# Block products as pairs of 64 by 64 tiles in a recurrent mixer, and level products of a gated recurrence issued one step later

## What is computed

```python
def step(state, inp):
    r_t, w_t, k_t, v_t, a_t, b_t = inp
    sa = jnp.einsum('bhvk,bhk->bhv', state, a_t)
    state = (state * w_t[:, :, None, :] + sa[..., None] * b_t[:, :, None, :]
             + v_t[..., None] * k_t[:, :, None, :])
    return state, jnp.einsum('bhvk,bhk->bhv', state, r_t)
```

## Time and profile before

| | us |
|---|---|
| median of three runs (lowest, highest) | 2407.83 (2401.4, 2412.27) |
| profiled execution, its own time | 2398.57 |
| span of the profiled execution | 2396.8 |
| PE busy in it | 2364.5 (99%) |
| DVE, ACT, POOL busy | 1660.5, 1274.0, 384.4 |

### The profile page before, as it was taken

One profiled execution on the slowest core, in us unless ns is written; L12 is line 12 of the kernel. 1 busy time (PEld: TensorE's weight loads), 2 busy tenths in 40 slices (PEclk: granted clock), 3 DMA queues, 4 the chain that ended last, 5 costly groups with the idle time before them and its releaser, 6 DMA issues.

```text
span 2396.8 us, 50331 instructions
## 1 busy us (share of the span) xinstructions
PE 2364.5 (99%) x21468; PEld 2299.1 (96%) x21468; DVE 1660.5 (69%) x2312; ACT 1274.0 (53%) x1816; POOL 384.4 (16%) x327
## 2 busy tenths in 40 slices
PE   9999999999999999999999999999999999999998
PEld 9999889999999999899999999989999999989998
DVE  7775776966667657878666765776666666777664
ACT  6554656645445456565554444655554454655553
POOL 4012020300200210203003002521002002521001
PEclk9999999999999999999999999999999999999999
DMA  7555433555555554245554555412555555412553
GB/s 256 188 194 192 159 126 137 178 194 193 189 183 193 192 178 174 107 142 186 199 192 179 220 194 195 155 53 103 199 194 183 198 188 193 164 57 90 211 188 129
DMA packets 57679, 410.18 MB, mean 171 GB/s; under 512 B 6384, under 2 KB 6640, under 8 KB 8688
## 3 DMA queue, kind: packets, MB, share of 16 engines
q1 hardware_dynamic: 56592, 402.15, 46.4%
q10 hardware_dynamic: 864, 4.82, 0.6%
HBM read 405.89 MB, written 1.05 MB: 170 GB/s over the span
## 4 chain that ended last, share of the span: by engine, by line
PE 88%; DVE 6%; ACT 3%; issue 2%; DMA 0%; DVEq 0%; SPq 0%; POOL 0%; POOLq 0%; ACTq 0%
PE bank L301 87%; DVE area L314 3%; ACT area L310 3%; DVE sb_wlo L314 2%; PE bank L305 1%; DVE area L342 1%; ACT sb_whi L310 0%; DVE area L325 0%; ACT L310 0%; DMA sb_x<-x 0%; DVE area L352 0%; DVE sb_x L325 0%; DVE area L320 0%; DVE area L319 0%; DVE sb_x L314 0%
## 5 line engine op out<-in xcount | busy, mean ns | idle before, releaser
L301 PE MATMUL bank<-area,sb_whi 128*128 128x256 f32 x11752 | 2041.3, 279 | 5.2 <-ACT area L310 3.1
L301 PEld LDWEIGHTS bank<-area,sb_whi 128*128 128x128 f32 x11752 | 1781.1, 188 | 17.7 <-ACT area L310 5.2
L301 PE MATMUL bank<-area,sb_wlo 128*128 128x256 f32 x5876 | 1620.2, 278 | 4.1 <-DVE sb_wlo L314 4.0
L310 ACT ACTIVATE sb_whi<-sb_raw 128x1024 fp32r<-128x1024 f32 x762 | 799.7, 1057 | 710.3 <-PE bank L301 705.8
L301 PEld LDWEIGHTS bank<-area,sb_wlo 128*128 128x128 f32 x5876 | 1101.1, 188 | 5.6 <-DVE sb_wlo L314 5.6
L314 DVE TENSOR_TENSOR sb_wlo<-sb_raw,sb_whi 128x1024 fp32r<-128x1024 f32 x762 | 962.4, 1272 | 166.1 <-ACT sb_whi L310 164.6
L314 DVE TENSOR_TENSOR area<-area,area 128x256 f32<-128x256 f32 (+6 forms) x502 | 257.9, 523 | 233.4 <-ACT area L310 231.9
L310 ACT ACTIVATE area<-area 128x256 f32<-128x256 f32 (+6 forms) x515 | 252.3, 498 | 81.9 <-DVE area L314 63.2
L314 DVE TENSOR_TENSOR area<-bank,sb_x_diag 128x512 f32<-128x512 f32 x244 | 166.8, 684 | 31.4 <-PE bank L301 18.8
L301 PE MATMUL bank<-area,area 64*64 64x64 f32 (+4 forms) x2496 | 154.9, 248 | 8.3 <-ACT area L310 6.0
L301 PEld LDWEIGHTS bank<-area,area 64*64 64x64 f32 (+3 forms) x2496 | 130.8, 149 | 28.3 <-ACT area L310 9.6
(11 more groups left out here) (82 smaller groups left out, 704.2 us busy)
## 6 DMA issues: line engine op xcount, KB each, us to landing
sb_raw<-stream SPq DMA_DIRECT2D x379, 1024.0 KB, 4.8
sb_raw<-stream SPq DMA_DIRECT2D x4, 512.0 KB, 7.7
area<-lora ACTq DMA_DIRECT2D x2, 768.0 KB, 4.8
area<-c ACTq DMA_DIRECT2D x1, 1504.0 KB, 8.4
sb_x<-x SPq DMA_DIRECT2D x4, 256.0 KB, 5.8
area<-mem ACTq DMA_DIRECT2D x1, 1024.0 KB, 7.2
out<-sb_x SPq DMA_DIRECT2D x4, 256.0 KB, 2.9
area<-m ACTq DMA_DIRECT2D x1, 512.0 KB, 3.7
```

The source lines that it names most:

```text
L301: return lambda e: e.matmul(out, lhsT, rhs, start=start, stop=stop, skip_group_check=True, tile_position=at)
L310: return lambda e: e.activation(out, a, f, **kw)
```

## The change

Every block-diagonal operand goes. `own_head` multiplies the two halves of the partitions apart, as 64 by 64 tiles at rows and columns 0 and 64, both into the same PSUM bank, on the lower and the upper half of its partitions. The clears on POOL, the copies onto diagonals on ACT and the pairs of half-height operations on DVE go with the arrays. `rwkv_inverse` starts with the pending evacuation (`settle`) and with bank 3 (`m.turns = 0`), and the transposes of `at` move from its start into its first two rounds, on bank 7. In the first mixer the level products of a step are issued in the next step, behind its values and ahead of its filler; the four scalings of `decays` move to `k.later`; the sum `soft` moves from POOL to DVE.

```diff
@@ attend
+    products = None
     for s in range(14):
...
         if 0 <= s - 2 < 12:
             values_of(s - 2)
+        if products:
+            products()
         if s < 12:
             exponentials(s, n)
...
         fill(k)
-        if products:
-            products()
@@ recurrence
+        def lowered():
+            dve.wait(pool, w.clipped)
+            dve.wait(act, n2)
+            for h in range(4):
+                w.lowered = dve.mark(tensor_scalar(z[:, h, :], zp[:, h, :], -1.0, ALU.mult,
...
+        k.later.extend((exponentials, logs, lowered))
     def decays():
-        dve.wait(pool, w.clipped)
...
-        pool.wait(dve, w.c_start)
-        w.soft = pool.mark(tensor_tensor(flat(zp), flat(zp), flat(e1), ALU.add))
+        def soft():
+            w.soft = dve.mark(tensor_tensor(flat(zp), flat(zp), flat(e1), ALU.add))
+        k.later.append(soft)
@@ the new helper
+def own_head(k, out, lhsT, rhs, start=True):
+    for e in range(2):
+        r = half_of(e)
+        n = k.pe.mark(matmul(out[r], lhsT[r], rhs[r], start=start, stop=True, at=(64 * e, 64 * e)))
     return n
@@ wide_products
-        n = k.pe.mark(matmul(k.bank[b][:, 128 * j:128 * j + 128], lhs[:, 4 * i + j, :], rhs[:, 4 * i + j, :]))
+        g = 4 * i + j
+        n = own_head(k, k.bank[b][:, 128 * j:128 * j + 128], lhs(g), rhs[:, g, :])
@@ rwkv_inverse
+    settle(k)
+    m.turns = 0
...
-        for e in range(2):
-            n = dve.mark(tensor_tensor(m.ak_d[half_of(e), groups(i), half_of(e)], broad(k, b)[half_of(e), :, 64:128],
-                                       wide(const2(k, "lower"), 4)[half_of(e)], ALU.mult))
+        done["ak"] = dve.mark(tensor_tensor(m.ak[:, groups(i), :], broad(k, b)[:, :, 64:128],
+                                            wide(const2(k, "lower"), 4), ALU.mult))
...
-    rwkv_by_token(k, m, m.at, m.a_tm_d, done["at"], "a_tm")
     for n in range(1, 6):
...
+        if n <= 2:
+            pe.wait(*m.freed[7])
+            done["a_tm"] = rwkv_by_token(k, k.bank[7], n - 1, m.at, m.a_tm)
+            m.freed[7] = (act, done["a_tm"])
         fill(k, 1)
...
-            if n < 5:
-                x_done[h] = dve.mark(tensor_tensor(by_row(xx, h), product, by_row(xx, h), ALU.add))
-            else:
-                for e in range(2):
...
+            x_done[h] = dve.mark(tensor_tensor(by_row(xx, h), product, by_row(xx, h), ALU.add))
@@ rwkv_chunks
         s_done = act.mark(activation(flat(m.st[i]), b[:, 0:256], ACT.Copy))
...
-        act.wait(act, s_done)
-        for e, r in enumerate(rows_):
-            d_done = act.mark(activation(m.st_d[r, groups(i), 64 * e:64 * e + 64], m.st[i][r], ACT.Copy))
...
-        pe.wait(act, d_done)
+        pe.wait(act, s_done)
```

More of the change, by code:

```diff
@@ L2061, in rwkv_prepare @@
     first[0](first[1])
-    pool.wait(pe, before)
-    for a in m.diag[:3]:
-        clear(a)
     two("k", kk, 2, 8)
@@ L2246, in rwkv_prepare @@
     flush_later(k)
-    act.wait(pool, w.cleared)
-    rwkv_by_token(k, m, v, m.v_tm_d, done["v", 2], "v_tm", center=True)
+    pe.wait(dve, done["v", 2])
+    for tt in range(2):
+        u = side_bank(k, m)
+        done["v_tm"] = rwkv_by_token(k, k.bank[u], tt, v, m.v_tm, center=True)
+        m.freed[u] = (act, done["v_tm"])
     bonus_products()
-    k.later.extend((k_diagonal, bonus, rotate))
+    k.later.extend((bonus, rotate))
     plain(k, m, ("rg", 0), m.rg[:, 0:2, :])
@@ L2253, in rwkv_prepare, with rwkv_by_token @@
     flush_later(k)
[L2255 to L2277, removed]
+def rwkv_by_token(k, bank, tt, src, dst, center=False):
+    for j in range(4):
+        to, block = bank[:, 128 * j:128 * j + 128], src[:, j, 128 * tt:128 * tt + 128]
+        n = k.pe.mark(matmul(to, block, const(k, "center")) if center else transpose(to, block, const(k, "ident")))
+    k.act.wait(k.pe, n)
+    for c in range(2):
+        for e in range(2):
+            read = bank[half_of(c)].rearrange("p (j c) -> p j c", j=4)[:, :, half_of(e)]
+            n = k.act.mark(activation(dst[half_of(e), groups(2 * tt + c), :], read, ACT.Copy))
+    return n
 def rwkv_products(k, m, name, i, unit=False):
@@ L2301, in rwkv_inverse @@
     x_done, t_done, w_done, a_done = {}, {}, {}, {}
-    at_of = lambda g: m.at[:, g % 4, 64 * (g // 4):64 * (g // 4) + 64]
+    settle(k)
+    m.turns = 0
     dve.wait(k.c2_slot, k.c2_in)
-    pe.wait(act, max(done["bt", "d"], done["at", "d"]))
-    dve.wait(pool, max(m.cleared, done["xx"]))
+    pe.wait(dve, max(done["bt"], done["at"], done["kt"]))
+    dve.wait(pool, done["xx"])
     for h in range(2):
         b = side_bank(k, m)
-        n = block_products(k, b, h, m.bt_d, at_of)
+        for o in range(8):
+            g = 8 * h + o
+            n = own_head(k, k.bank[b][:, 64 * o:64 * o + 64], m.bk[:, g, 0:64], at_of(m, g))
         dve.wait(pe, n)
@@ L2417, in own @@
             o = 64 * (4 * (i % 2) + j)
-            in_halves(k, ys[i // 2][:, o:o + 64], m.v_tm_d[:, 4 * i + j, :], m.rk[:, 4 * i + j, 0:64],
-                      start=i % 2 == 0 and j == 0, stop=False)
+            own_head(k, ys[i // 2][:, o:o + 64], m.v_tm[:, 4 * i + j, :], m.rk[:, 4 * i + j, 0:64],
+                     start=i % 2 == 0 and j == 0)
     def squares(h, bank, n):
```

85 lines of the change are left out of this document (23 added, 62 removed).

## The result

The changed kernel takes 2376.76 us in the median of four executions (2376.17 to 2378.21), the kernel before 2410.05 in as many (2401.40 to 2413.69). The ratio is 0.9876, with a 95% interval of 0.985 to 0.9902: faster by 1.2%. The forecast was faster, but by 17 us, and its range ended at 2382; the kernel gained 33 us. The profiled execution, at 2377.26 us with a span of 2375.5, is 21.3 us under the one of before.

A forecast was written before the change was run, and what follows sets the result against it. PE, busy 99% of the span, was taken as the bound, so only its waits could be won: 5.4 + 2.5 + 9.0 = 16.9 us off 2407.8 gives 2391 us, range 2382 to 2408.

The forecast's parts named there:

- Part 3: Start of the inverse, second mixer: two PE waits cost 1.8 us, 0.25 left for bank 7, gain 1.5 us a layer.
- level products: First mixer: issuing them one step later removes all eight PE waits on DVE ahead of them, gain 5.4 us.
- decays: First mixer: moving scalings and the sum removes PE's 1.10 us wait for a weights split in two layers, gain 2.5 us.
- second mixer: Start and end of the inverse plus the chain: 4.5 us a layer, 9.0 us for both layers.
- the second rival: Waits return at values or a split in the first mixer: 11.5 us gain stays, 2396 us, chance 0.16.
- the case that I called the worst: At `decays`, the sum on DVE stays beside the two splits: DVE needs 3.7 us in place of 4.2.
- Parts 3 and 4: Second mixer: start of the inverse 1.5 us, its end 1.2, the chain 1.7; together 4.5 us a layer.
- Part 5: Second mixer's 64 by 64 tiles: no gain, no loss taken; upper bound 57.7 us if tiles run in turn.
- The chain: Chain behind the inverse: dropping ACT's two copies shortens two PE waits of 0.93 us, gain 1.7 us a layer.
- the work taken from POOL and ACT: POOL's clears and ACT work away from the priced places: counted as nothing, since PE waits for neither there.
- The rival of tiles in turn: Two tiles of one product in one bank take turns: +57.7 - 16.9 = +41 us, 2449 us, chance 0.12.

The follow-up runs named there:

- E4: Kernel before with only the decays edits (four scalings moved to `k.later`, sum `soft` on DVE): 2404.14 us median (2396.22 to 2415.00).
- E6: Kernel before with only the new start of the inverse, all block-diagonal arrays kept: twelve executions between 2396.07 and 2399.11 us.
- E10: Changed kernel plus six ACT copies that the first round's second quarter products wait for: four executions at 2379.37 to 2380.51 us, two at 2385.45 and 2386.64.
- E2: Kernel before with only the first mixer's edits (level products a step later, scalings to `k.later`, sum on DVE): 2392.22 us median, profile span 2387.8.
- E3: Kernel before with only the second mixer's edits (64 by 64 tiles, no block-diagonal arrays, new order of the inverse): 2388.01 us, span 2385.2.
- E5: Changed kernel with the old start of the inverse, 64 by 64 tiles kept: five executions 2384.51 to 2390.37 us; a sixth, 4821.82 us, left out.
- E7: Changed kernel with two ACT copies behind every state of the chain put back, for which PE waits: 2380.99 us (2380.66 to 2383.76).
- E11: Changed kernel plus four ACT copies that the first round's second quarter products wait for: five executions between 2377.96 and 2379.15 us.

## Why the prediction was wrong

**The step that failed is the price of the waits in Part 3.** It made the two waits at the inverse's start 1.8 us, their idle time and the overlap, and took the clock as 1.00 because the one profile showed that. Half of the executions of before (39 of 79) have a mean clock of 0.996 or less. In E4's trace of such an execution the engine fell to 1.2 GHz from about there, and the same work took 6 and 9 us more in the two layers. E6 took away the second of these waits and left 0.65 us of the first kind, and the executions of low clock went; E10 put a wait of 1.26 us in the second one's place, and two of six returned. The sum of the forecast was made against an execution of full clock and then set off the median of executions that, by their times, mostly weren't. So the 33.3 us between the medians are 21.3 between the profiles, and 11.5 by which the median of before (2410.05) lies over its profile (2398.57); 0.5 is the change's own (2377.26 to 2376.76). The size of the 11.5 is luck: over the 79 executions the median lies 3.4 us over that profile. The range failed with this step: its lower end counted all idle time, and a fall of the clock isn't idle.

**The terms between executions of full clock** were right in place in the main, level products and second mixer too small:

| | forecast | measured by |
|---|---|---|
| level products | 5.4 | 6.5: E2's span (9.0) less decays |
| decays | 2.5 | 2 x 1.27: dense products around the place |
| second mixer | 9.0 | 12.6: dense products ahead of and behind the two mixers, before and after |
| sum | 16.9 | 21.6; 21.3 from profile to profile |

E3's span shows 11.6 for the second mixer, since its profiled execution lost 2 us in its first 60 us, where the two kernels do the same.

*Level products:* seven of the eight waits went; the last is 0.23 us where it was 0.30. In addition steps without a wait got 0.3 us shorter (one from 3.57 to 3.28 us between a low part of one filler and a low part of the next, at 318 and 317 us), likely because the products now start beside the last values. What the second rival named, waits that come back at a split, happened on a small scale: 1.0 us in three waits of the second layer. E2 has them too, E4 not, so they come with the level products.

*Decays:* as forecast, in the case that I called the worst: the sum does stand between the splits, and DVE is early enough. PE had waited for the first of the two slow splits, which alone took 3.07 us.

*Second mixer:* the stretch over the inverse fell from 49.8 to 46.3 us, 3.5 where Parts 3 and 4 have 1.5 + 1.2. The waits of the earlier trace rows at both ends went: 1.8 + 0.8 + 0.4, less 0.43 for bank 7, where 0.25 was left: 2.6. Bank 7 was thus dearer than Part 3 allowed. Of the other 0.9 a part is Part 5, where I excluded a gain: the tiles are cheaper by 0.004 us a group, and, it seems, tiles of one size follow each other without the pause that a change of size makes: the group products ahead of the rounds took 9.43 us in the timeline of before (128 records) and 9.07 in E5's (192 records for the same). What is left of the 0.9 wasn't followed. The chain gave 1.78 for 1.74 (E7). Some 0.5 us a layer was won ahead of the inverse, between dense products, where the forecast put the work taken from POOL and ACT at nothing; in the third layer a wait of 0.30 us for a split, at 1540.25 us, is gone there. Why was not tested.

**The rival of tiles in turn fell** with the first trace: 0.219 us a group, twice that by that rival. The rule on row tiles and banks that I weighed in Part 5 doesn't hold for tiles on different halves of the partitions of a bank; the measurement decides. It fits a sentence of another page of the Trainium skill, "PSUM — Partial Sum Buffer", section "PSUM bank collisions raise a hardware error", which says that each bank in each partition is a memory of its own; the same section also repeats the rule that fell here. Row halves in one bank and on the same partitions weren't tried.

**Still open:** why the clock falls in some executions and not in others of the same kernel, and whether the first wait of 0.49 us has a share in it beside the second. E5 had one wait of 1.73 us and a low clock in five executions of five, though in its trace in only one of the two layers; before has 0.49 and 1.16 and a low clock in half, E10 0.36 and 1.26 and in two of six, E11 0.36 and 0.39 in none of five, E6 one wait of 0.65 in none of twelve.

## What to carry to other kernels

When the timed executions of a kernel spread and its profile sits at the fast end, look at the granted clock of every execution before summing waits: the profile may be of the kind that doesn't show the cost. A wait of a microsecond between small tiles can cost several times its idle time (E10: 1.26 us, and some 6 more in two of six executions); two waits of 0.93 us in the chain (E7) cost no more than the forecast's 1.74. Block-diagonal operands are not needed to keep two small heads side by side: here two tiles on the diagonal cost PE no more (0.219 us a group for 0.223) and spare the other engines the zeros.

## What the runs showed of the hardware

- In the traces of E4 and E5 the clock fell to 1.2 GHz within 3 us behind a wait of 1.16 to 1.73 us, on an engine that was 99% busy, and stayed there for 10 to 20 us; behind a like wait in E5's fourth layer it did not. With waits of 0.39 us (E11) or 0.65 us (E6) at the start of the rounds no execution showed a low clock.
- Two tiles of 64 by 64 on different halves of the rows, in one bank and on different halves of its partitions, ran side by side: 0.219 us a group.
- DVE was slower beside POOL: two splits took 4.20 us beside POOL's sum, and 1.22 each without it.
- Tiles of 64 by 64 issued four of one half and then four of the other cost under a fifth of what taking turns would (1.3 of 8 x 0.87 us).
